# Second block's feed-forward: the first two chunks evicted together, four up-projections and then three down-projections at its end

## What is computed

```python
def second_block(x, ...):
    for l in range(DEPTH):                       # DEPTH = 2
        ...                                      # attention and Fourier mixing, x = x + mix @ w_o
        h = rmsnorm_2(x, norm2[l])
        up = dwconv_centred(h @ w_up[l], conv_w[l], conv_b[l])   # width 3, along the sequence
        gate, val = up[..., :D_FF_2], up[..., D_FF_2:]           # D_FF_2 = 2816
        x = x + (jax.nn.silu(gate) * val) @ w_down[l]
    return x

def dwconv_centred(h, w, bias):
    hp = jnp.pad(h, ((0, 0), (1, 1), (0, 0)))
    return hp[:, :-2] * w[0] + hp[:, 1:-1] * w[1] + hp[:, 2:] * w[2] + bias
```

## Time and profile before

| what | value |
|---|---|
| median of 3 runs | 2029.85 us (2028.68 to 2032.68) |
| the profiled execution, its time | 2035.71 us |
| its span | 2033.9 us |
| PE busy | 1957.6 us, 96% of the span |
| DVE busy | 1534.1 us, 75% |
| ACT busy | 1039.3 us, 51% |
| mean granted TensorE clock | 0.986 of full |
| second block's feed-forward, layer 1 | 1537 to 1734 us |
| second block's feed-forward, layer 2 | 1835 to 2030 us |

### The profile page before, as it was taken

The page is one execution under the profiler, slowest core; times in us unless marked ns, Lnnn a source line. Parts: engine busy times, 40 slices in busy tenths (PEclk is TensorE's granted clock), DMA queues, the critical chain, the costliest instruction groups (busy, mean ns, idle before and its releaser), DMA issues.

```text
span 2033.9 us, 38986 instructions
## 1 busy us (share of the span) xinstructions
PE 1957.6 (96%) x15906; PEld 1884.5 (93%) x15906; DVE 1534.1 (75%) x2207; ACT 1039.3 (51%) x1322; POOL 0.2 (0%) x4
## 2 busy tenths in 40 slices
PE   7999999799999999999997999999999999998998
PEld 7999998689999999999986899999889999888998
DVE  6556899997755575568999977555787777878776
ACT  5444545366544444445554665444465555555554
POOL 0000000000000000000000000000000000000000
PEclk9999999899999999999998999999999999999999
DMA  6555555224655445565552246555235554334553
GB/s 247 195 186 217 188 196 183 87 73 146 217 203 186 169 145 186 186 217 187 197 187 82 74 152 222 186 186 178 95 124 174 198 186 165 118 140 150 198 193 135
DMA packets 55817, 343.38 MB, mean 169 GB/s; under 512 B 7328, under 2 KB 7584, under 8 KB 18976
## 3 DMA queue, kind: packets, MB, share of 16 engines
q1 hardware_dynamic: 54704, 339.37, 47.8%
q10 hardware_dynamic: 1008, 2.51, 0.3%
HBM read 334.51 MB, written 1.05 MB: 165 GB/s over the span
## 4 chain that ended last, share of the span: by engine, by line
PE 73%; DVE 20%; ACT 4%; DMA 2%; issue 1%; DVEq 0%; ACTq 0%; SPq 0%
PE bank L433 23%; PE bank L434 23%; PE bank L435 23%; DVE lo L1558 6%; DVE cv L1759 6%; ACT hi L1052 2%; DMA raw<-in_w 1%; DVE p_sb L1738 1%; DVE qk L1732 1%; DVE n_lo L1562 1%; DMA x<-in_x 1%; DVE sq L1592 0%; DVE zr L1722 0%; PE bank L821 0%; DVE zg L1721 0%
## 5 line engine op out<-in xcount | busy, mean ns | idle before, releaser
L1558 DVE TENSOR_TENSOR lo<-raw,hi 128x2048 fp32r<-128x2048 f32 (+1 forms) x336 | 715.5, 2131 | 221.2 <-ACT hi L1052 220.6
L433 PE MATMUL bank<-n_hi,hi 128*128 128x256 f32 x2256 | 639.4, 283 | 29.0 <-DVE lo L1786 12.4
L1052 ACT ACTIVATE hi<-raw 128x2048 fp32r<-128x2048 f32 (+1 forms) x336 | 598.3, 1783 | 109.0 <-PE bank L435 92.6
L434 PE MATMUL bank<-n_lo,hi 128*128 128x256 f32 x2256 | 633.0, 281 | 0.0
L435 PE MATMUL bank<-n_hi,lo 128*128 128x256 f32 x2256 | 632.9, 281 | 0.0
L433 PEld LDWEIGHTS bank<-n_hi,hi 128*128 128x128 f32 x2256 | 432.9, 192 | 34.9 <-DVE lo L1786 12.4
L434 PEld LDWEIGHTS bank<-n_lo,hi 128*128 128x128 f32 x2256 | 427.0, 189 | 1.2 <-issue 1.0
L435 PEld LDWEIGHTS bank<-n_hi,lo 128*128 128x128 f32 x2256 | 426.7, 189 | 0.0
L433 PE MATMUL bank<-h_hi,hi 128*128 128x256 f32 x1152 | 336.7, 292 | 4.7 <-DVE h_lo L1562 4.7
L434 PE MATMUL bank<-h_lo,hi 128*128 128x256 f32 x1152 | 328.0, 285 | 0.0
L435 PE MATMUL bank<-h_hi,lo 128*128 128x256 f32 x1152 | 327.8, 285 | 0.0
(11 more groups left out here) (242 smaller groups left out, 2230.1 us busy)
## 6 DMA issues: line engine op xcount, KB each, us to landing
raw<-in_w SPq DMA_DIRECT2D x286, 1024.0 KB, 4.8
raw<-in_w SPq DMA_DIRECT2D x53, 512.0 KB, 4.0
zr<-zg SPq DMA_DIRECT2D x96, 64.0 KB, 2.9
bv<-in_bv SPq DMA_DIRECT2D x2, 768.0 KB, 6.2
spread<-in_spread SPq DMA_DIRECT2D x2, 768.0 KB, 8.0
x<-in_x ACTq DMA_DIRECT2D x4, 256.0 KB, 10.1
out_x<-sq SPq DMA_DIRECT2D x1, 1024.0 KB, 3.9
const<-in_const ACTq DMA_DIRECT2D x1, 831.5 KB, 13.6
```

Source lines behind the costliest of these rows:

```text
L433: mm(out, w_hi, a_hi, start=start, stop=False, skip_group_check=True)
L434: mm(out, w_hi, a_lo, start=False, stop=False, skip_group_check=True)
L1052: fn(hi[:, s, 0:w], raw[:, s, 0:w], ACT.Copy).then_inc(sem["hi"], 1)
L1558: v.tensor_tensor(lo[:, s, 0:w], raw[:, s, 0:w], hi[:, s, 0:w].bitcast(F32), ALU.subtract)\
```

## The change

Five things change, all in hand-written order:

1. At the start of the second block's feed-forward, DVE evicts both first chunks one behind the other. ACT does the split of the fourth chunk (`cb + 3`) ahead of `tap0(0)`, then both taps. DVE then does the low part of that chunk, both convolutions, both products, and `hidden(0)`.
2. The last four up chunks stand in a row, and behind them the last three down chunks. The loop of pairs is one round shorter on each engine.
3. The second last pair now uses `last_hi` and `last_lo`, and the last pair uses new tiles `end_hi` and `end_lo`, in space that is free there.
4. `summed_stat` moves inside the second up chunk: behind 3 input tiles instead of 2 in the second block, behind 4 instead of 2 in the very first feed-forward of the kernel. The other feed-forwards of the first block keep theirs.
5. The weights are laid out in memory in the new order (`_ffn_chunks`), so the DMAs are the same in number and size.

The number of matmuls, splits and elementwise instructions is the same.

```diff
@@ pe_program, ffn
-            pairs(cb + 1, bank[1], 0, KT, n_hi, n_lo, True, stat_after=2)
+            pairs(cb + 1, bank[1], 0, KT, n_hi, n_lo, True, stat_after=4 if by_halves else 2 if early else 3)
...
+            times = PAIRS - 3 if early else PAIRS - 4
...
+            else:
+
+                c = cb + FFN_CHUNKS - 7
+                for j in range(4):
+                    take("up")
+                    pairs(c + j, bank[j % 2], 0, KT, n_hi, n_lo, True)
+                down(c + 4)
+                down(c + 5, False, last_hi, last_lo)
+                last_down(c + 6, norm_follows, end_hi, end_lo)
@@ act_program, ffn2
             scaled_std()
+            split(cb + 3)
             tap0(0, lambda q: col(P2, "conv", q))
-            split(cb + 3)
+            tap0(1, lambda q: col(P2, "conv", 8 + q))
             silu2(0)
             hidden(0)
-            tap0(1, lambda q: col(P2, "conv", 8 + q))
             silu2(1)
...
-            c = cb + FFN_CHUNKS - 4
+            c = cb + FFN_CHUNKS - 7
             split(c + 2)
-            tap0(0, lambda q: col(P2, "conv", 16 * (PAIRS - 1) + q))
+            tap0(0, lambda q: col(P2, "conv", 16 * (PAIRS - 2) + q))
             hidden(1)
             split(c + 3)
             silu2(0)
             last_hidden(0)
-            tap0(1, lambda q: col(P2, "conv", 16 * (PAIRS - 1) + 8 + q))
+            tap0(1, lambda q: col(P2, "conv", 16 * (PAIRS - 2) + 8 + q))
+            split(c + 4)
             silu2(1)
             last_hidden(1)
-            split(c + 4, half_chunk_2(0))
-            split(c + 5, half_chunk_2(1))
+            tap0(0, lambda q: col(P2, "conv", 16 * (PAIRS - 1) + q))
+            split(c + 5)
+            silu2(0)
+            end_hidden(0)
+            tap0(1, lambda q: col(P2, "conv", 16 * (PAIRS - 1) + 8 + q))
+            split(c + 6)
+            silu2(1)
+            end_hidden(1)
+            split(c + 7, half_chunk_2(0))
+            split(c + 8, half_chunk_2(1))
@@ dve_program, ffn2
             up(0, pe_after(cb), ub[:, 0, :, 1:S + 1])
+            up(1, pe_after(cb + 1), ub[:, 1, :, 1:S + 1])
             split(cb + 3)
             conv3(0, lambda q: col(P2, "conv", q))
+            conv3(1, lambda q: col(P2, "conv", 8 + q))
             product(0, c3)
-            up(1, pe_after(cb + 1), ub[:, 1, :, 1:S + 1])
+            product(1, c3)
             hidden(0)
-            conv3(1, lambda q: col(P2, "conv", 8 + q))
-            product(1, c3)
@@ _ffn_chunks
+    if not early:
+        out = out[:-6] + ups[-4:] + downs[-3:-1]
     return out + [downs[-1]]
```

More of the change, by code:

```diff
@@ L497, in down_tile, with down @@
                        tile(lo, c, 8 * k + m), h_hi[:, k, :], h_lo[:, k, :], start=start)
-        def down(c, first=False):
+        def down(c, first=False, of_hi=hid_hi, of_lo=hid_lo):
             take("lo")
@@ L504, in down, with last_down @@
                 for m in range(KT):
-                    last = down_tile(c, k, m, hid_hi, hid_lo, start=first and k == 0 and m % 2 == 0)
+                    last = down_tile(c, k, m, of_hi, of_lo, start=first and k == 0 and m % 2 == 0)
                 last.then_inc(sem["half" if k == 0 else "pe"], 1)
-        def last_down(c, norm_follows):
+        def last_down(c, norm_follows, of_hi, of_lo):
             take("lo")
@@ L514, in last_down @@
                 for k in range(2):
-                    last = down_tile(c, k, m, last_hi, last_lo)
+                    last = down_tile(c, k, m, of_hi, of_lo)
                 if m % 2:
@@ L537, in ffn @@
             pairs(cb, bank[0], 0, KT, n_hi, n_lo, True, ready="h", by_halves=by_halves)
-            pairs(cb + 1, bank[1], 0, KT, n_hi, n_lo, True, stat_after=2)
+            pairs(cb + 1, bank[1], 0, KT, n_hi, n_lo, True, stat_after=4 if by_halves else 2 if early else 3)
             cnt.up("sq", 4)
+            times = PAIRS - 3 if early else PAIRS - 4
             two_tiles(True)
-            with pe.Fori(0, PAIRS - 3) as i:
+            with pe.Fori(0, times) as i:
                 before = cnt.enter(i, per)
                 two_tiles(False)
-                cnt.leave(before, PAIRS - 3)
-            c = cb + FFN_CHUNKS - 4
-            take("up")
-            pairs(c, bank[0], 0, KT, n_hi, n_lo, True)
-            take("up")
-            pairs(c + 1, bank[1], 0, KT, n_hi, n_lo, True)
-            down(c + 2)
-            last_down(c + 3, norm_follows)
+                cnt.leave(before, times)
+            if early:
+                c = cb + FFN_CHUNKS - 4
+                take("up")
+                pairs(c, bank[0], 0, KT, n_hi, n_lo, True)
+                take("up")
+                pairs(c + 1, bank[1], 0, KT, n_hi, n_lo, True)
+                down(c + 2)
+                last_down(c + 3, norm_follows, last_hi, last_lo)
+            else:
+                c = cb + FFN_CHUNKS - 7
+                for j in range(4):
+                    take("up")
+                    pairs(c + j, bank[j % 2], 0, KT, n_hi, n_lo, True)
+                down(c + 4)
+                down(c + 5, False, last_hi, last_lo)
+                last_down(c + 6, norm_follows, end_hi, end_lo)
             cnt.up("up", 2)
@@ L1108, in last_hidden, with end_hidden @@
             fn(last_hi[:, u, :], prod_t[:, u, :], ACT.Copy).then_inc(sem["hidhi"], 1)
+        def end_hidden(u):
+            take("prod")
+            fn(end_hi[:, u, :], prod_t[:, u, :], ACT.Copy).then_inc(sem["hidhi"], 1)
         def ffn1(cb):
@@ L1626, in last_hidden, with end_hidden @@
             low_part(last_lo[:, u, :], prod_t[:, u, :], last_hi[:, u, :], "hid")
+        def end_hidden(u):
+            take("hidhi")
+            low_part(end_lo[:, u, :], prod_t[:, u, :], end_hi[:, u, :], "hid")
         def add_to_x(b, p, factor):
```

42 lines of the change are left out of this document (27 added, 15 removed).

## The result

The changed kernel takes 2013.68 us (median of 6 runs, 2009.91 to 2019.2), the kernel before 2029.59 beside it (6 runs). The ratio is 0.9914, 95% interval 0.9886 to 0.9942, so 17.5 us (12 to 23) are gone where 21.1 were forecast. The ratios in this document are ratios of the mean times; the medians of this pair are 15.9 us apart. Further down, one run of 4022.8 us of `before_drained` and one of 3183.0 us of the kernel before beside it stand apart as slow ones and are left out. The profiled execution after has 2012.8 us, 2011.0 of them span.

What follows compares the result with a forecast made beforehand. PE, busy 96% of the span, bounds the kernel; time can be won only at its waits or low clock. Gains 6.1 + 5.3 + 0.1 + 2.7 + 2.7 + 1.7 + 2.5 = 21.1 us off 2029.85 give 2008.8, range 2005.5 to 2016.5.

Steps and rivals of the forecast that it cites:

- the sixth chunk: Start of the second block's feed-forwards: sixth chunk begins 17.8 us behind up(0), gaining 6.1 us in layer 2, 5.3 in layer 1.
- the last chunk at T + 33.16: End of each feed-forward, T the seventh last chunk's start: last chunk forecast at T + 33.15 instead of 35.87, 2.7 us each.
- evictions: DVE in the four up chunks at the end: evictions 6.2 us apart, against PE's 5.44 us a chunk.
- the last add: End of layer 2: last add starts 5.75 us behind the last chunk's start instead of 7.49, gaining 1.7 us.
- n_lo: End of layer 1: n_lo done 9.45 us behind the last chunk's start instead of 11.94, gaining 2.5 us.
- The new waits: PE waits the new order adds in each layer: 0.7 us at the fifth chunk, 0.5 at the last.
- Rival 1: The start's wait only moves to the fifth (down) chunk, 2.8 us instead of 0.7, with low clock behind: 2016.3 us; 10%.
- Rival 2: The clock still falls at one or two of the four starts and ends, costing 3.6 to 7.2 us: 2014.2 us; 17%.
- Rival 3: DVE slower through the four up chunks, evictions 8.3 us apart, last chunk 6.3 us later per layer: 2021.4 us; 5%.
- rival 4: Something other than the eviction holds the fourth chunk at the start, 11.4 us less gain: 2020.2 us; 4%.
- rival 5: Slower than before because DVE becomes the bound of the end; at 10.5 us a chunk 2034.5 us; 1%.

Runs made afterwards that it cites:

- before_drained: The kernel before, with PE waiting three times for its own last matmul in each feed-forward's first down chunk (18 waits): 2022.1 us, ratio 0.9971.
- splits_sooner: The kernel after, with the fifth chunk's high part (ACT) and the last chunk's low part (DVE) each one place sooner: 2017.1 us, ratio 0.9939 to the kernel before.
- start_only: The kernel before with only the change's start edits and the moved summed_stat, old end kept: 2024.2 us against 2030.6, ratio 0.9967.
- the drained pair: The kernels before and after, each with the same 18 added PE waits for its own matmul: 2022.1 and 2017.4 us; 21.2 us apart at the fast pace.
- drains: The kernel after, with PE waiting in every round of two hidden tiles for its own sixth matmul: 2015.3 us, ratio 0.9921 to the kernel before.

## Why the prediction was right

**The places.** Step by step against the profile after: the sixth chunk 17.95 us behind `up(0)` (17.8 forecast), the last chunk at T + 33.16 (33.15), evictions 6.2 apart (6.2), the last add 5.90 behind the last chunk (5.75), `n_lo` 9.6 (9.45). The timetables from measured durations, with 0.1 us of overlap for successive short DVE instructions, were good to 0.2 us.

**The new waits.** At the fifth chunk 0.28 us are listed, and in layer 1 it starts 0.4 later behind the third than in `splits_sooner`, where it doesn't wait (11.44 against 11.0); 0.7 was forecast. At the last chunk 0.26 us in layer 1 (33.16 against 32.90 with the earlier split), 0.5 forecast; in layer 2 none, since PE was slower there.

**Rival 1** (the wait only moves) needed 2.8 us at the fifth chunk: it fell. **Rival 2** (the clock still falls) fell with waits of 0.28 and 0.51 us and a clock of 1.00. What the Trainium skill, TensorE: Matmul & The Clock Gate, "A second HAM failure mode: psum-queue depth-cycling", says of frequent short idles was not seen here: none of the nine profiles that have the changed start and end shows a low stretch at the four places. **Rival 3** fell with the 6.2 us, **rival 4** with `start_only`, **rival 5** with both.

**The size.** The sum was 21.1, the ratio gives 17.5 (12 to 23), and the repeated runs of the same program 13.4 (8 to 19) and 15.0 (10 to 20). Two things were taken too lightly. The starts' 6.1 and 5.3 and the ends' 1.7 and 2.5 come from one profile, with the low stretches that it happened to have. Measured place by place, that profile gives 20.7 us and the second of before 18.7. And the sum was made as if PE had one pace. From layer 1's `up(0)` on, at the fast pace, the change is worth 22.0, 18.7 and 18.4 us (the third by the drained pair). So the mechanism and the places were right, and 21.1 is the upper part of what they give. The comparisons of the runs lie lower, at 13 to 17.5, but each of their intervals reaches 18.7 or more, so they don't contradict it. Whether after also spends more time at the slow pace than before, through the breaks that it removes ahead of the second block's streams, stays open: those two streams were slow in 4 of 16 cases in eight profiles with the new start, and in 1 of 8 in four with the old, too few to tell.

**Two readings that the sum didn't use.** A chunk wholly at the lower level was put at 3.3 us more. By the earlier trace rows a matmul takes 6.02 / 28 = 0.215 us there, so 48 of them take 4.9 us more. And rival 2 priced a low stretch of 6.8 us at 3.6, as if PE lost all of it; at layer 1's start one cost 0.75, since the fifth chunk had to wait for `lo` anyway.

The forecast of 2008.8 lies 4.9 below the median of 2013.68, within the range of 2005.5 to 2016.5. The upper end was drawn for the clock's rival, and no low clock came at the four places. What the sum left out was that it was taken from a profile with long low stretches, and the scatter by the pace, for which it had no term. That the range held both is luck in part.

## What to carry to other kernels

When the engine that bounds has a few waits of known cause, lay the measured durations out in the new order: the start times came out within 0.2 us. Before a gain is read from one pair of profiles, count the matmuls per 100 us in a stretch that wasn't changed; if that differs, or a low-clock stretch differs in length, take a second profile of the kernel before, and price an edit from both. A wait of 3 us can cost more than its length through the clock behind it, and how much more differs from one execution to the next: a low stretch ahead of another wait can cost nothing.

## What the runs showed of the hardware

- A stream of 128x256 float32r matmuls, each with its own weights, has two paces at the full granted clock, 113.5 and 117.8 ns (885 and 851 in 100 us). The pace holds from one break to the next, over up to 1524 matmuls, and differs between executions of the same program. An estimate by the Trainium skill, TensorE: Matmul & The Clock Gate, "Wait — 56ns, not 53.3ns?", where a start-to-start time is N / 2.4 GHz and some 2.5 ns, gives 256 / 2.4 + 2.5 = 109.2 ns. Both measured paces lie above that, and the measurement decides.
- PE's wait for its own matmul costs 0.33 us in `drains`.
- A stretch of low clock at one place varies between executions of the same kernel: 3.4 us or none at layer 2's start, 6.8 or 3.4 at layer 1's, each time with the same wait of 2.8 us for `ub`. A shorter wait can have one too: behind a wait of 1.93 us for `h_lo` between 1778 and 1811 us, which no version touches, 7 of the 14 profiles show a low stretch of 3.4 us and 7 none.
